# A two-layer hybrid encoder trunk: 512 columns moving in two projections, and x passed with its axes exchanged

## The reference

```python
for l in range(2):
    h = rmsnorm(x, norm_g[l])
    proj = h @ w_in[l]            # 1024 -> 7936 columns
    (a_q, a_k, a_v, a_gate, b_u, b_v, b_gate,
     c_q, c_f, c_i, c_gate, merge) = split(proj)
    out_a = sliding_window_attention(rope(a_q), rope(a_k), a_v, sinks) * silu(a_gate)
    out_b = spatial_gating(gelu(b_u), gelu(b_v), ...) * silu(b_gate)   # b_v: layer norm, 128x128 mixing
    f = lb + (1 - lb) * sigmoid(c_f)
    out_c = rmsnorm(hgrn2(c_q, 1 - f, c_i, log(f))) * silu(c_gate)     # c_i: the recurrence's values
    y = sum(sigmoid(merge + b_merge) * (branches @ w_branch[l])) @ w_out[l]
    x = x + y
return rmsnorm(x, final_g)
```

## Time and profile before

| | before |
|---|---|
| median of 3 runs | 1004.77 us (1004.13 to 1005.16) |
| the profiled execution | 1005.19 us |
| its span, first to last instruction | 1003.4 us |
| busy TensorE, VectorE, ScalarE, GpSimd | 993.5, 624.4, 496.8, 290.7 us |
| mean granted clock of TensorE | 0.997 |
| projections with 256 columns moving | 768 matmuls |

### The profile page before, as it was taken

One profiled execution on the slowest core, in us unless ns is written; L12 is line 12 of the kernel. 1 busy time (PEld: TensorE's weight loads), 2 busy tenths in 40 slices (PEclk: granted clock), 3 DMA queues, 4 the chain that ended last, 5 costly groups with the idle time before them and its releaser, 6 DMA issues.

```text
span 1003.4 us, 15882 instructions
## 1 busy us (share of the span) xinstructions
PE 993.5 (99%) x6662; PEld 839.5 (84%) x6662; DVE 624.4 (62%) x864; ACT 496.8 (50%) x833; POOL 290.7 (29%) x148
## 2 busy tenths in 40 slices
PE   8999999999999999999999999999999999999997
PEld 7888998888888888888888989988888888888886
DVE  6889976897535353536638798488954535353652
ACT  6976576665523232223366766566554232323333
POOL 2322215324313232324112121162243232223330
PEclk9999999999999999999999999999999999999999
DMA  6432232222133232324233222321222323232602
GB/s 225 123 111 63 75 106 84 84 75 89 32 102 102 87 121 79 115 70 140 85 116 102 68 85 87 105 85 55 80 98 81 109 77 110 67 120 82 195 1 84
DMA packets 91639, 94.73 MB, mean 94 GB/s; under 512 B 2272, under 2 KB 89520, under 8 KB 91568
## 3 DMA queue, kind: packets, MB, share of 16 engines
q1 hardware_dynamic: 91440, 93.68, 29.8%
q10 hardware_dynamic: 128, 0.04, 0.0%
HBM read 91.62 MB, written 2.10 MB: 93 GB/s over the span
## 4 chain that ended last, share of the span: by engine, by line
PE 98%; issue 0%; DVE 0%; ACT 0%; POOL 0%; DVEq 0%; ACTq 0%; POOLq 0%
PE pj L537 29%; PE pj L539 28%; PE pj L538 28%; PE mx L537 2%; PE mx L538 2%; PE mx L539 2%; PE mx L637 1%; PE mx L737 1%; PE mx L614 1%; PE mx L683 1%; PE mx L711 1%; PE mx L622 1%; PE mx L714 1%; PE mx L701 1%; PE mx L496 0%
## 5 line engine op out<-in xcount | busy, mean ns | idle before, releaser
L1191 POOL TENSOR_TENSOR w_lo<-w_raw,w_hi 128x1024 fp32r<-128x1024 f32 (+1 forms) x89 | 197.9, 2224 | 546.7 <-ACT w_hi L855 546.7
L537 PE MATMUL pj<-h_hi,w_hi 128*128 128x512 f32 x832 | 328.2, 394 | 0.0
L539 PE MATMUL pj<-h_hi,w_lo 128*128 128x512 f32 x832 | 324.2, 390 | 0.0
L538 PE MATMUL pj<-h_lo,w_hi 128*128 128x512 f32 x832 | 324.0, 389 | 0.0
L855 ACT ACTIVATE w_hi<-w_raw 128x1024 fp32r<-128x1024 f32 (+1 forms) x179 | 159.0, 937 | 163.6 <-PE pj L539 163.6
L1302 DVE TENSOR_TENSOR w_lo<-w_raw,w_hi 128x1024 fp32r<-128x1024 f32 (+1 forms) x90 | 173.1, 1923 | 81.1 <-ACT w_hi L855 80.8
L537 PEld LDWEIGHTS pj<-h_hi,w_hi 128*128 128x128 f32 x832 | 156.2, 188 | 33.1 <-issue 1.4
L539 PEld LDWEIGHTS pj<-h_hi,w_lo 128*128 128x128 f32 x832 | 156.2, 188 | 33.0
L538 PEld LDWEIGHTS pj<-h_lo,w_hi 128*128 128x128 f32 x832 | 156.3, 188 | 31.2
L1412 DVE TENSOR_TENSOR merge_gate<-pj,rstd 128x512 f32<-128x512 f32 x48 | 33.2, 691 | 164.5 <-PE pj L539 164.5
L973 ACT ACTIVATE merge_gate<-merge_gate,small 128x512 f32<-128x512 f32 x48 | 34.3, 715 | 92.7 <-DVE merge_gate L1412 92.7
(11 more groups left out here) (270 smaller groups left out, 1416.1 us busy)
## 6 DMA issues: line engine op xcount, KB each, us to landing
w_raw<-in_w_in SPq DMA_DIRECT2D x61, 1024.0 KB, 5.5
w_raw<-in_w_branch SPq DMA_DIRECT2D x24, 512.0 KB, 3.4
w_raw<-in_w_out SPq DMA_DIRECT2D x6, 1024.0 KB, 5.2
x_tokens<-in_x SPq DMA_DIRECT2D x4, 512.0 KB, 6.6
w_raw_last<-in_w_out SPq DMA_DIRECT2D x2, 1024.0 KB, 7.4
sp_wT<-in_sp_w SPq DMA_DIRECT2D x2, 512.0 KB, 3.7
out<-out_low SPq DMA_DIRECT2D x4, 256.0 KB, 2.0
out<-out_high SPq DMA_DIRECT2D x4, 256.0 KB, 2.3
```

The costliest lines, as they stand in the source:

```text
L537: pe.matmul(bank, wh, ah, start=first, stop=False)
L538: pe.matmul(bank, wh, al, start=False, stop=False)
L539: return pe.matmul(bank, wl, ah, start=False, stop=final)
L1191: return pool.tensor_tensor(out=dst, in0=full, in1=hi.bitcast(f32), op=ALU.subtract)
```

## The change

In `ci` and `bv` the two units of a kind now hold the rows k 0 to 3 and k 4 to 7 of all 512 columns, instead of 256 columns each, and each of their four jobs takes one block of 128 positions with 512 weight columns moving. The second unit of each (`ASIDE`) has a buffer of its own for high parts (`WHX`), and both raw buffers are held until the fourth job. ci 1 stands directly behind ci 0. Where the weights of ci 1, cq 1, bv 1 and ag 1 are split is written out (`PREP` and entries in the lists).

x is also passed transposed (`xT`), and the four small vectors come transposed in one array (`vecs`). x's own pieces in token order, for the statistics, are loaded behind unit 2; the statistics, the diagonal and the sines' products stand in VectorE's phase 3, and TensorE waits for `p_diag` behind job 3. The norm is multiplied into cos and sin once. In each layer VectorE evacuates the first job of mix 11 ahead of the weights that it splits there.

```diff
-         + [(k, p) for p in range(2) for k in ("cf", "cq", "ci")]
+         + [("cf", 0), ("cq", 0), ("ci", 0), ("ci", 1), ("cf", 1), ("cq", 1)]
...
+WIDE = [(UNITS.index((k, 0)), UNITS.index((k, 1))) for k in ("ci", "bv")]
+for _a, _b in WIDE:
+    JOBS_TO[_a] = JOBS_TO[_b]
+ASIDE = [b for _, b in WIDE]
+PREP = {FIRST[UNITS[u - 1]]: u for u in range(1, NU + 1) if UNITS[u % NU] not in (("ci", 1), ("cq", 1), ("bv", 1), ("ag", 1))}
+PREP.update({FIRST[("cf", 1)] + 1: UNITS.index(("cq", 1)),
+             FIRST[("bv", 0)] - 1: UNITS.index(("bv", 1)), FIRST[("ag", 0)] + 1: UNITS.index(("ag", 1))})
...
+STEPS = (dict(clamp=8, forget=8, keys=9, ...), dict(clamp=18, forget=20, keys=21, ...))
...
@@ sync @@
             sp.dma_start(CST[:, :], consts[:, :]).then_inc(cst_in, 16)
-            load_x(0)
+            load_xT(0)
             sp.dma_start(buf[:, 0:2, :], src[:, 0:2, :]).then_inc(first_in[0], 16)
-            load_x(1)
+            load_xT(1)
+            load_xT(2)
...
             load_weights(sp, 2)
+            for j in range(KT // 2):
+                load_x(j)
...
@@ tensor @@
-            warm(4)
-            pe.wait_ge(cst_in, 16)
-            pe.wait_ge(norm_in, 16)
-            pe.transpose(M[1][:, 0:16], VN[0:16, :], CST[0:16, 0:16]).then_inc(normT_done, 1)
-            warm(5)
-            transpose_x(0)
-            transpose_x(1)
-            pe.wait_ge(vec_in, 16 * 3)
-            pe.transpose(PJ[2][:, 0:64], VR[0:64, :], CST[0:64, 0:64]).then_inc(vecT_done, 1)
-            pe.wait_ge(p_norm, 1)
+            warm(10)
+            small_warm(22)
...
-                        for b in range(2):
-                            tok = slice((2 * t + b) * P, (2 * t + b + 1) * P)
-                            for k in range(KT):
-                                last = three(bank[:, b * UC:(b + 1) * UC], ah[:, k, tok], al[:, k, tok],
-                                             wh[:, k, :], wl[:, k, :], k == 0, k == KT - 1)
+                        first = layer * NU + u - i
+                        tok = slice((2 * i + t) * P, (2 * i + t + 1) * P)
+                        for k in range(KT):
+                            v = first + k // 4
+                            if n == FIRST[(kind, 0)] and k == 4:
+                                pe.wait_ge(w_lo, v + 1)
+                                pe.wait_ge(w_lo_vec, v + 1)
+                            c = slice(k % 4 * T, (k % 4 + 1) * T)
+                            last = three(bank[:, :], ah[:, k, tok], al[:, k, tok], hi_of(v)[:, c], WLO[:, slot(v), c],
+                                         k == 0, k == KT - 1)
...
+                    pe.wait_ge(rope_done, upto(rope_done, j + 2))
                     if j == 0:
-                        pe.wait_ge(rope_done, upto(rope_done, 5))
...
-                    if n == 2 and layer == 0:
-                        pe.wait_ge(xT_evac, KT)
-                        pe.wait_ge(fill_done, 1)
+                    if n == 3 and layer == 0:
                         pe.wait_ge(p_diag, 1)
...
@@ scalar @@
+                    if p == 0:
+                        phase[at_["forget"]].append((split_hi, layer * NU + ASIDE[0]))
+                    phase[at_["forget"]].append((forget, p))
...
@@ vector @@
-                    dve.tensor_tensor(out=R1[:, :], in0=QR[:, r % 3, :], in1=COS[:, :], op=ALU.mult)
-                    chained(dve.tensor_tensor(out=R2[:, :], in0=QS[:, r % 3, :], in1=SIN[:, :], op=ALU.mult))
-                    chained(dve.tensor_tensor(out=R1[:, :], in0=R1[:, :], in1=R2[:, :], op=ALU.add))
-                    dve.tensor_tensor(out=dst, in0=R1[:, :], in1=RS[:, :], op=ALU.mult).then_inc(rope_done, 1)
+                    dve.tensor_tensor(out=R1[:, :], in0=QR[:, r % 3, :], in1=COSR[:, :], op=ALU.mult)
+                    chained(dve.tensor_tensor(out=R2[:, :], in0=QS[:, r % 3, :], in1=SINR[:, :], op=ALU.mult))
+                    dve.tensor_tensor(out=dst, in0=R1[:, :], in1=R2[:, :], op=ALU.add).then_inc(rope_done, 1)
...
-                    phase[0].append((rstd_diagonal,))
+                    phase[0].append((x_stats, 0))
                     phase[0].append((angle_rest,))
-                    phase[2].append((trig,))
+                    phase[3].append((statistics,))
+                    phase[3].append((rstd_diagonal,))
+                    phase[3].append((trig,))
...
+                phase[STEPS[0]["keys"]].append((split_lo, layer * NU + ASIDE[0]))
...
+                phase[STEPS[0]["first_taken"]].append((split_lo, layer * NU + UNITS.index(("cq", 1))))
...
+                    if n == FIRST[("mix", 11)]:
+                        evac(n)
                     if due:
                         split_lo(v)
                     if layer == DEPTH - 1 and n in (FIRST[("mix", 10)] + 1, FIRST[("mix", 11)]):
                         split_lo(LAST_OUT + (n > FIRST[("mix", 10)] + 1))
-                    if n < NJ:
+                    if n < NJ and n != FIRST[("mix", 11)]:
                         evac(n)
```

More of the change, by code:

```diff
@@ L349, in jobs_to, with hi_turn, hi_of, hi_user @@
             return v // NU * NJ + JOBS_TO[v % NU]
+        def hi_turn(v):
+            layer, u = divmod(v, NU)
+            return layer * (NU - len(ASIDE)) + u - sum(a < u for a in ASIDE)
+        def hi_of(v):
+            if v % NU in ASIDE:
+                return WHX[ASIDE.index(v % NU)][:, :]
+            return WHI[:, hi_turn(v) % WB, :]
+        def hi_user(v):
+            return max(w for w in range(v) if w % NU not in ASIDE and hi_turn(w) == hi_turn(v) - WB)
         def raw_of(v):
@@ L941, in evac @@
                         dst, fn = (VC, ACT.Copy) if kind == "ci" else (GV, ACT.Gelu_apprx_tanh)
[L942 to L946 removed]
+                        tb = 2 * i + t
+                        act.activation(dst[:, tb, :], src, fn, scale=RT[:, tb:tb + 1]).then_inc(done, 1)
                 def values():
@@ L1237, in program @@
                 phase = {n: [] for n in range(NJ + 4)}
+                phase[FIRST[("cq", 0)]].append((split_lo, layer * NU + ASIDE[0]))
                 phase[23].append((ln_affine,))
@@ L1245, in program @@
                 for n in range(NJ + 4):
-                    v = layer * NU + JOBS[n][0] + 1 if n < NJ and JOBS[n][1] == 0 else 0
+                    v = layer * NU + PREP.get(n, -NU)
                     if 1 < v < LAST_OUT:
@@ L1332, in _ @@
             first_low(1)
-            x_stats(0)
             first_low(2)
@@ L1336, in _ @@
             first_low(3)
-            x_stats(1)
+            first_low(4)
             split_half(0, 1)
-            first_low(4)
             first_low(5)
-            x_stats(2)
             first_low(6)
+            dve.wait_ge(w_hi, 3)
+            dve.tensor_tensor(out=lo_part(1, 0), in0=raw_part(1, 0), in1=hi_part(1, 0).bitcast(f32),
+                              op=ALU.subtract).then_inc(w_lo, 2)
             first_low(7)
-            split_lo(1)
-            pchain(x_stats(3))
-            for tb in range(TB):
-                last = dve.bn_aggr(MV[:, tb, :], XS[:, tb, :, :])
-            pchain(last)
-            pchain(dve.tensor_tensor(out=MS, in0=MV[:, :, 0], in1=MV[:, :, 0], op=ALU.mult))
-            dve.tensor_tensor(out=MS, in0=MS, in1=MV[:, :, 1], op=ALU.add).then_inc(p_ms, 1)
-            dve.wait_ge(p_vec, 1)
+            split_half(1, 1)
+            dve.wait_ge(lb_in, 16)
             L0, L1, mx = LBT[:, 24:28], LBT[:, 28:32], LBT[:, 0:4]
@@ L1364, in trig, with statistics @@
                 dve.wait_ge(p_trig, 1)
+            def statistics():
+                for j in range(1, KT // 2):
+                    last = x_stats(j)
+                pchain(last)
+                for tb in range(TB):
+                    last = dve.bn_aggr(MV[:, tb, :], XS[:, tb, :, :])
+                pchain(last)
+                pchain(dve.tensor_tensor(out=MS, in0=MV[:, :, 0], in1=MV[:, :, 0], op=ALU.mult))
+                dve.tensor_tensor(out=MS, in0=MS, in1=MV[:, :, 1], op=ALU.add).then_inc(p_ms, 1)
             def rstd_diagonal():
@@ L1818, in program @@
                         continue
-                    v = layer * NU + JOBS[n][0] + 1 if n < NJ and JOBS[n][1] == 0 else 0
+                    v = layer * NU + (PREP[n] if n in PREP and UNITS[PREP[n] % NU] != ("cq", 1) else -NU)
                     early = n <= FIRST[("cf", 0)] or n < NJ and JOBS[n][0] >= UNITS.index(("merge", 0)) - 1
+                    early = early and n not in (STEPS[1]["khat"] + 2, FIRST[("mix", 11)])
                     if 1 < v < LAST_OUT and early:
```

161 lines of the change are left out of this document (70 added, 91 removed).

## The result

| | before | after |
|---|---|---|
| median | 1004.96 us (4 runs, 1004.13 to 1005.40) | 1012.76 us (4 runs, 1011.00 to 1013.16) |
| span of the profiled execution | 1003.4 us | 1009.0 us |
| mean granted clock in it | 0.997 | 0.992 |

The ratio is 1.0076, with a 95% interval of 1.0063 to 1.0089: slower by 0.8%, and 7 us over the forecast of 1005.5. The profiled execution took 1011.0 us and is the shortest of the four; the clock in the others was 0.990.

The account below looks back on a forecast made before the run. The prediction took TensorE's instruction stream plus a start and a tail as the bound. Its terms, -4.7 + 1.5 + 2.0 + 0.6 + 1.3 = +0.7, took the median from 1004.77 to about 1005.5 us, 8-in-10 range 999 to 1009.5.

Parts of the forecast that it names:

- the first part: The prediction's opening section on what bounds the kernel: TensorE's instruction stream plus a start and a tail.
- Width, -4.7: ci and bv jobs: 384 matmuls of 512 columns replace 768 of 256, taking 4.7 us off TensorE's path.
- the row was taken and not the rule: Width: timeline paces (0.120 and 0.2273 us) gave 4.7 us; the skill's 2.5 ns issue gap would give 1.0.
- Opening, +1.5: Start through job 4: 4.6 us gained, then lost waiting for p_diag, later if VectorE meets GpSimd; clock fall adds 1.7.
- The gain is given back: Opening: p_diag's lateness starts job 4 at 36.7, against 36.9 before, despite 4.6 us gained in jobs 0 and 1.
- stays covered: Opening: k's rope waits for rstd behind ScalarE's split of unit 3, but jobs 4 and 5 move with it.
- cq 1 and ag 1, +2.6: Middle of both layers: TensorE waits for late low halves, 1.0 per layer at cq 1, 0.3 at ag 1.
- rival (a): Middle has slack: both waits vanish, sum -1.9, or -3.9 (about 1001.5) with a better opening; chance 0.29.
- Tail, +1.3: Before layer 1's output projection: the last weight split ends 1.3 us later behind product and sum; bounds 0 and +3.0.
- the 0.3 us there stays about the same: Layer 0's tail: evacuating mix 11's first job ahead of the weight split replaces one 0.3 us wait by another.
- (c): Slower rival: the clock falls after each new hole, at cq 1's waits and the tail, 1.7 each; 1010, chance 0.24.
- (b): Faster rival: the statistics aren't late, so the opening keeps its 4.6; 995.5, or 998 with middle waits; chance 0.07.

Follow-up runs that it names:

- experiment 5: Changed kernel with cq 1's load, and bv 0's behind it, held for the scores behind job 13, some 2 us later; 1005.59 us, ratio to before 1.0008.
- experiment 10: Experiment 5 with each wide ci and bv matmul cut into two of 256 columns, on the same operands; 1010.05 us, ratio to before 1.0047.
- experiment 1: Changed kernel with bv 0's weights loaded one job later; 1012.31 us, ratio to before 1.0072.
- experiment 2: Changed kernel with 16 more small matmuls before the first projection; 1005.58 us in one run.
- experiment 4: Changed kernel with the last weights' low parts made ahead of the evacuation of mix 11's first job, as before the change; 1009.61 us, ratio to before 1.0044.
- experiment 6: Changed kernel with 4 more small matmuls before the first projection; 1012.27 us in one run.
- experiment 3: Changed kernel with the norms' spreading and TensorE's wait for the diagonal behind job 4 instead of job 3; 1009.68 us, ratio to before 1.0051.
- experiment 8: Changed kernel with the edits of experiments 3, 4 and 5, plus two ropes, the keys' swap and the values moved later; 1006.13 us, ratio to before 1.0015.
- experiment 9: Experiment 8 with cq 0's weights split one phase sooner in the opening and the values a phase later; 1001.25 us, ratio to before 0.9958.

## Why the prediction was wrong

**The step that failed** is the premise of the first part, that "a change counts in two ways only: it takes TensorE work out, or it makes TensorE wait for an operand that used to be in time". There is a third: TensorE waits for its own instructions. It has no term in the sum and no rival, and it is worth 3.3 us and a fall of the clock, 5.1 in the profile shown; experiment 5 gives back 7.2 in the medians. Without it the time is 1005.6, beside 1005.5 forecast. That is luck: the errors of the other terms cancel.

**Width, -4.7:** right, 4.5 (experiment 10). That the row was taken and not the rule was right. The sum slipped a little: 5.76 less 5.46 is 0.30 for a job and not 0.295, which makes 4.9.

**Opening, +1.5:** mis-sized, +2.9 in the profile shown, (bounds by their own terms -1.3 and +3.1, not -1.5 and +3.3), and 3.4 to 4.2 in the profiles of the six experiments (1, 2, 4, 5, 6, 10) that have the same opening, but for some small matmuls in two of them, with a longer fall of the clock. p_diag came at 36.8, outside the bounds of 34.2 to 36.5 and 1.5 later than the 35.3 that I took. 1.2 of that is the choice between the bounds: the meeting with GpSimd came, as the upper one had it. The table loads were missing from the chain: the root waited 0.8 for the second, of which 0.5 was covered by steps shorter than I had summed. "Job 4 starts at 36.7" became 39.8: these 1.5, and the fall of the clock, which I had priced at 1.7 behind it and which fell on the norm_sum (2.07 for 0.89) and the transposes (0.85 for 0.44). "The gain is given back" was right, and experiments 3, 8 and 9 show how deep it goes: behind the wait for the diagonal stands a second one for cq 0's weights, and behind that the softmax. I had written that k's rope "stays covered"; it was so only while TensorE was late itself.

**cq 1 and ag 1, +2.6:** wrong, 0.15 at cq 1 of layer 1 and else 0. In layer 1 cq 1's half was ready at 607.8, 1.3 us sooner than my sum (603.9, and 5.2 for the later layer): the softmax ahead of it, which I had 0.5 us later for ScalarE's split, came 0.7 sooner. It is the difference of two sums near each other, and the rival (a) described it.

**Tail, +1.3:** right for the hole; the fall behind it, which I had as an upper bound, came too, and experiment 4 gives 3.15 back. But "the 0.3 us there stays about the same", said of layer 0, did not hold: the wait for `product` (0.27 at 459.33 before) is gone and 0.15 gained.

The terms as measured in the profiles, -4.5 + 2.9 + 3.0 + 5.1, make +6.5, and the span grew by 5.6. The ends of the jobs place what is between: 0.15 at the end of layer 0, and 0.35 in each layer behind job 36, where the matmuls of the state (L711 before) had started 0.2 late and slower (in layer 0, 253.42 to 256.56, beside 258.90 to 261.94). Why they don't now is not shown. **The rivals:** (c) came nearest, 1010 for 1012.8, with the right price of a fall but mostly at other places, since the waits for cq 1 did not come. (b) was right to want the statistics sooner, though with them in time the softmax is next.

The rule on the interface shared with GpSimd ("VectorE: DVE Perf Modes", "Two Vector instructions with no wait between them", in the Trainium skill) agrees again: 2.78 us for 0.60, at a spot where it lay in the chain.

What stays open: what decides whether the clock falls behind a hole of 1.7 to 2.0 us, and how long it stays low behind a longer one, and so how the 7.2 us of experiment 5 divide. Nor was it tried to have the requests for instructions fall elsewhere in each layer; the kernel of experiment 9 still has a stop of 0.4 us there.

## What to carry to other kernels

Where TensorE runs through hundreds of tiny matmuls in a few microseconds, it can run dry of instructions, and a large load issued by the end of the job just before holds up its fetch: look for a wait put down to "issue" that no semaphore explains, find the instruction queue's packet in the DMA view, and start the load a little later. A few matmuls more or less anywhere ahead can move a kernel by 0.7%, so an A/B of two orders should be read from the trace before the order is blamed. And a wait that is taken away shows the one that it covered: undo one, look, and undo the next, until the sum of the chain on the other engines is shorter than TensorE's own.

## What the hardware did that I had not expected

- The 16 KB packets of the instruction queue stand one to some 256 instructions (49 packets for 12,580 loads and matmuls of TensorE, 52 for the 13,348 of experiment 10). The packet at job 13 came 1.7 us behind that job's end with no load in flight and 4.7 us with one, and TensorE went on 2.3 to 2.9 us after it in the kernels that stopped there.
- Behind each of 14 holes of 2.98 us and more the granted clock was at 0.50, the lower level of 1.2 GHz, and was up again 3.5 to 6.0 us after the hole's end. Behind holes of 0.5 to 1.23 us it never fell, and once not behind 2.4 us in the start. Of thirteen holes between 1.66 and 2.0 us it fell behind six, the same 1.94 us at the tail going both ways.
- A wait that was filled with useless matmuls kept the clock at 1.00 (2.4 GHz) and brought job 7 forward by 2.9 us.
